# Differential attention whose key and query units hold both maps of two heads, with later projections between its rounds

## The reference

```python
kv = jnp.einsum('bsd,de->bse', kvh, w_kv)      # k1 | k2 | v, 6 heads of 64, 64 and 128
q1 = proj[..., :DIFF_QK].reshape(b, s, DIFF_HEADS, DIFF_HEAD_DIM)
q2 = proj[..., DIFF_QK:2 * DIFF_QK].reshape(b, s, DIFF_HEADS, DIFF_HEAD_DIM)
qm = proj[..., 2 * DIFF_QK:]                   # queries of the memory, 4 heads of 64
q1 = partial_rope(rmsnorm_2(q1, b_q_norm[j]), cos, sin)     # k1, k2, q2 likewise
s1 = jnp.einsum('bqhd,bkhd->bhqk', a1, k1).astype(jnp.float32) * scale
p = (p1 - lam * p2).astype(v.dtype)            # p1, p2: softmax of the maps s1, s2
o = rmsnorm_2(o, b_subln[j], SUBLN_EPS) * (1.0 - lam_init)
mo = memory_attention(qm, mem_n, w_mem_kv[l], mem_q_norm[l], mem_k_norm[l])
x = x + jnp.einsum('bse,ed->bsd', jnp.concatenate([main, mo], axis=-1), w_o[l])
```

## Time and profile before

| | us |
|---|---|
| median of 3 runs | 1164.06 |
| lowest and highest run | 1162.13, 1166.34 |
| the profiled execution, its own time | 1163.43 |
| its span | 1161.6 |
| mean granted clock of TensorE | 0.966 |

### The profile page before, as it was taken

How to read it: one execution, slowest core, us unless ns; L and a number is a source line. 1 busy time by engine, 2 the same in 40 slices (tenths; PEclk the granted TensorE clock), 3 DMA queues, 4 the chain that set the end, 5 groups by cost and what they waited for, 6 DMA issues and landing times.

```text
span 1161.6 us, 19998 instructions
## 1 busy us (share of the span) xinstructions
PE 1086.9 (94%) x8646; PEld 1061.7 (91%) x8646; DVE 650.1 (56%) x833; ACT 542.5 (47%) x770; POOL 371.0 (32%) x198
## 2 busy tenths in 40 slices
PE   6889898999899999989999999999999669999998
PEld 6889898899899999979999999999997559999998
DVE  3767755556684654555755444447555655544444
ACT  3366675543556444533355343445434334553341
POOL 2436256231464433450001341221531020252121
PEclk9989999899899999989999999999999689999999
DMA  9978457545377555434355555564433104655540
GB/s 325 279 243 254 133 165 257 171 146 177 114 250 258 181 182 179 148 121 133 111 181 199 177 190 181 173 211 163 146 114 106 36 1 146 218 182 180 183 146 37
DMA packets 167715, 197.38 MB, mean 170 GB/s; under 512 B 5283, under 2 KB 139852, under 8 KB 167500
## 3 DMA queue, kind: packets, MB, share of 16 engines
q1 hardware_dynamic: 167628, 196.11, 52.2%
HBM read 195.03 MB, written 1.06 MB: 169 GB/s over the span
## 4 chain that ended last, share of the span: by engine, by line
PE 71%; DVE 11%; ACT 8%; DMA 3%; issue 3%; POOL 2%; SPq 2%; DVEq 1%; ACTq 0%; POOLq 0%
PE bank L486 70%; DVE w_lo L1525 4%; ACT w_hi L1029 3%; DMA ada_raw<-in_w_ada 2%; ACT ada_raw L1019 2%; ACT probs L1092 1%; SPq L442 1%; DVEq L1941 1%; POOL ada_raw L1384 1%; DVE y_tok L1648 1%; DMA probsT<-in_buckets 1%; DVE big L1921 0%; DVE probs L1629 0%; DVE h_lo L1582 0%; DVE big L1747 0%
## 5 line engine op out<-in xcount | busy, mean ns | idle before, releaser
L1525 DVE TENSOR_TENSOR w_lo<-w_raw,w_hi 128x2048 fp32r<-128x2048 f32 x158 | 389.0, 2465 | 283.7 <-ACT w_hi L1029 283.1
L486 PE MATMUL bank<-h_hi,w_hi 128*128 128x256 f32 x1328 | 382.2, 293 | 13.4 <-DVE w_lo L1525 11.1
L486 PE MATMUL bank<-h_hi,w_lo 128*128 128x256 f32 x1328 | 377.3, 289 | 0.0
L1029 ACT ACTIVATE w_hi<-w_raw 128x2048 fp32r<-128x2048 f32 x158 | 301.3, 1908 | 133.0 <-PE bank L486 124.2
L486 PE MATMUL bank<-h_lo,w_hi 128*128 128x256 f32 x1328 | 346.4, 286 | 1.3 <-POOL h_lo L1353 1.3
L486 PE MATMUL bank<-u_hi,w_hi 128*128 128x256 f32 x1024 | 289.7, 286 | 8.9 <-DVE xT L1950 4.6
L486 PE MATMUL bank<-u_hi,w_lo 128*128 128x256 f32 x1024 | 287.3, 284 | 0.0
L1353 POOL TENSOR_TENSOR u_lo<-fresh,u_hi 128x512 fp32r<-128x512 f32 x60 | 139.1, 2320 | 453.0 <-ACT u_hi L1038 452.8
L486 PEld LDWEIGHTS bank<-h_hi,w_hi 128*128 128x128 f32 x1328 | 264.2, 199 | 16.6 <-DVE w_lo L1525 12.3
L486 PE MATMUL bank<-u_lo,w_hi 128*128 128x256 f32 x1024 | 277.2, 284 | 0.0
L486 PEld LDWEIGHTS bank<-h_hi,w_lo 128*128 128x128 f32 x1328 | 264.0, 199 | 0.0
(11 more groups left out here) (235 smaller groups left out, 1042.3 us busy)
## 6 DMA issues: line engine op xcount, KB each, us to landing
w_raw<-in_w_mlp SPq DMA_DIRECT2D x32, 1024.0 KB, 5.4
w_raw<-in_w_up SPq DMA_DIRECT2D x32, 1024.0 KB, 5.5
w_raw<-in_w_down SPq DMA_DIRECT2D x32, 1024.0 KB, 5.0
w_raw<-in_w_in SPq DMA_DIRECT2D x21, 1024.0 KB, 5.3
ada_raw<-in_w_ada SPq DMA_DIRECT2D x19, 1024.0 KB, 7.8
w_raw<-in_a_w_in SPq DMA_DIRECT2D x10, 1024.0 KB, 5.1
w_raw<-in_w_o SPq DMA_DIRECT2D x8, 1024.0 KB, 4.9
w_raw<-in_w_kv SPq DMA_DIRECT2D x6, 1024.0 KB, 5.3
```

Source lines behind the costliest of these rows:

```text
L486: return pe.matmul(dst, lhsT, rhs, start=start, stop=stop, skip_group_check=True)
L1029: act.activation(w_hi[:, n % PARTS_RING, :], w_raw[:, slot_of[n], :], ACT.Copy).then_inc(hi_w, 1)
L1525: dve.tensor_tensor(w_lo[:, n % PARTS_RING, :], w_raw[:, slot_of[n], :], w_hi[:, n % PARTS_RING, :].bitcast(F32), ALU.subtract).then_inc(l ...
```

## The change

A unit of keys or of queries now holds 128 columns of the first map and 128 of the second: both maps of two heads (`heads_unit`). The units come in the order k0, q0, v0, memory queries, k1, q1, v1, k2, q2, v2, and head pair 0 can start after k0 and q0. The six rounds begin there. The other units, the values and the two pairs of the memory's attention stand between the steps of the rounds, in the programs of all engines. The scores of the next round stand behind the transposition of this one, not ahead of it, and use two banks instead of four.

The gain of a key or query is applied where ACT empties the bank, the rotation follows at once, and only keys get their rstd multiplied in (`head_scale`, after the rotation). The rstd of queries (the first layer's memory queries too) goes into the scale of the exponential, and DVE multiplies it into the negated maximum. The five `spread_qk` of queries (q0, q1, q2 and both layers' memory queries) and their DVE multiplications are gone; those of the keys and of the memory's keys remain.

```diff
+    def heads_unit(name, src, pair):
+        n_unit(name, src, 0, "a", [(0, P * pair, P), (P, DIFF_HEADS * HD + P * pair, P)])
+
+    heads_unit("k", w["w_kv"], 0)
+    heads_unit("q", w["b_w_q"][0], 0)
+    n_unit("v", w["w_kv"], MAIN_W, "a")
+    n_unit("qm1", w["b_w_q"][0], MAIN_W, "a")
...
-            spread_qk("qm0", acc[3])
...
-            product_two(N_K, h_hi, h_lo, in_order(X_KV), ready=(x_hi, x_lo))
+            product(N_K[0], h_hi, h_lo, job=X_KV, ready=(x_hi, x_lo))
             sum_x("sum6")
...
+            product(N_Q[0], u_hi, u_lo, job=X_MIX1, ready=(x_hi, x_lo))
...
+            qk_squares("k0", N_K[0])
+            rotate("k0", tiles_of("k0"))
+            product_tok(N_V[0], h_hi, h_lo)
+            rotate("q0", tiles_of("q0"))
+            qk_squares("q0", N_Q[0])
+            spread_qk("k0", acc[3])
+            product(N_QM1, u_hi, u_lo)
+            d_scores(0)
+            product(N_K[1], h_hi, h_lo)
+            qk_squares("qm1", N_QM1)
+
+            d_turn(0)
+            d_scores(1)
+            qk_squares("k1", N_K[1])
+            rotate("k1", tiles_of("k1"))
+            pv(0)
+            product(N_Q[1], u_hi, u_lo)
+
+            d_turn(1)
+            spread_qk("k1", acc[3])
+            rotate("q1", tiles_of("q1"))
+            qk_squares("q1", N_Q[1])
+            pv(1)
+            turn_o(0)
+            product_tok(N_V[1], h_hi, h_lo)
+            d_scores(2)
+            product(N_K[2], h_hi, h_lo)
+
+            d_turn(2)
+            qk_squares("k2", N_K[2])
+            rotate("k2", tiles_of("k2"))
+            d_scores(3)
+            pv(2)
+            turn_o(1)
+            product(N_Q[2], u_hi, u_lo)
...
+            product_tok(N_V[2], h_hi, h_lo)
+            d_scores(4)
+            o_part(0, J_DIFF[0], first=True)
+            pe.wait_ge(spread_read, spread_no["qk.k2"] + 1)
+            m_scores(0)
+
+            d_turn(4)
+            d_scores(5)
+            pv(4)
+            turn_o(3)
+            m_turn(0)
+            m_pv(0)
+            m_scores(1)
+
+            d_turn(5)
+            m_turn(1)
+            pv(5)
+            turn_o(4)
+            m_pv(1)
+            o_part(1, J_DIFF[1])
+            pe.wait_ge(misc_read, misc_no["mem1.1"] + 1)
+            pe.wait_ge(d_max, DIFF_HEADS)
+            to_T(acc[0:1], y_tok, y_turned)
+            turn_o(5)
+            o_part(3, J_YM1)
...
+                act.activation(dst, lin[lin_bank[n]][:, :], ACT.Copy, scale=1.0 if gain is None else vec[:, gain:gain + 1])
...
+                                              scale=root[:, q_rstd:q_rstd + 1],
...
+            split_w(N_QM0)
             squares_x("sum3")
             squares_x("sum3g")
-            split_w(N_QM0)
...
+            d_exps(2)
+            split_w(N_K[2] + AHEAD)
+            evac_k(2)
+
+            d_copy(2)
+            d_exps(3)
+            o_square(2)
+            split_w(N_Q[2] + AHEAD)
+            evac_q(2)
...
+            d_copy(4)
+            d_exps(5)
+            mem_exps(0)
+            o_square(4)
+            split_w(N_V[2] + AHEAD + 1)
+            split_h(J_DIFF[1], u_hi, 2)
+            copy_turned("mem1.", 0, G_M1, 512, mem_pT)
...
+            d_maxima(2)
+            split_w(N_K[2] + AHEAD)
+            mix(2)
+
+            head_mean("k2")
+            rope_add("k2", k_pair[2])
+            d_maxima(3)
+            o_copy(2)
+            o_take(1)
+            split_w(N_Q[2] + AHEAD)
+            o_mean(2)
+            mix(3)
+            o_scale(2)
```

More of the change, by code:

```diff
@@ L650, in spread_qk @@
                 pe.wait_ge(root_ready, power_no[name] + 1)
-                if bank is ps_ada:
+                if bank is not acc[1]:
                     pe.wait_ge(spread_read, spread_no[name])
@@ new lines, in o_part @@
+            def o_part(pair, job, first=False, last=False):
+                for m in range(2):
+                    if first:
+                        start_unit(N_O1 + m)
+                    pe.wait_ge(fresh_lo, job + 1)
+                    part(N_O1 + m, pair, u_hi, u_lo, first=first, last=last)
+            qk_squares("k0", N_K[0])
[3 more added lines that the diff above has]
+            qk_squares("q0", N_Q[0])
@@ new lines, in _ @@
+            pv(3)
+            turn_o(2)
+            product_tok(N_V[2], h_hi, h_lo)
[15 more added lines that the diff above has]
+            m_pv(1)
@@ new lines, in _ @@
+            evac_q(0)
+            split_w(N_V[0] + AHEAD)
+            evac_v_unit(0)
+            split_w(N_QM1 + AHEAD)
+            evac_qk("qm1", N_QM1, v_tok[:, 0, :], gain=V_MQ + 1)
+            d_exps(0)
+            split_w(N_K[1] + AHEAD)
+            evac_k(1)
+            d_copy(0)
+            d_exps(1)
+            split_w(N_Q[1] + AHEAD)
+            o_square(0)
+            evac_q(1)
+            d_copy(1)
+            o_square(1)
+            split_w(N_V[1] + AHEAD)
+            evac_v_unit(1)
@@ L2013, in _, with head_mean @@
[L2013 to L2022 removed]
+            def head_mean(name):
+                mean_square("qk." + name, mix_eps)
@@ L2084, in o_take @@
                     dve.drain().then_inc(fresh_ready, 1)
-            y_copy(J_YM1, 0, 6)
-            split_w(N_O1 + AHEAD)
-            d_maxima(0)
-            for h in range(DIFF_HEADS):
-                mix(h)
-                if h >= 2:
-                    o_take(h - 2)
-                if h >= 1:
-                    o_mean(h - 1)
-                if h + 1 < DIFF_HEADS:
-                    d_maxima(h + 1)
-                if h >= 1:
-                    o_scale(h - 1)
-                o_copy(h)
@@ new lines, in _ @@
+            dve.tensor_scalar(stat[:, S_NLAM:S_NLAM + 1], stat[:, S_NLAM:S_NLAM + 1], -LAM_INIT, None, ALU.add)
+            head_scale(0)
+            split_w(N_V[0] + AHEAD)
+            dve.wait_ge(root_ready, power_no["qk.q0"] + 1)
+            d_maxima(0)
+            split_w(N_QM1 + AHEAD)
+            mix(0)
+            head_mean("qm1")
+            d_maxima(1)
+            split_w(N_K[1] + AHEAD)
+            head_mean("k1")
+            rope_add("k1", k_pair[1])
+            o_copy(0)
@@ new lines, in _ @@
+            split_w(N_Q[1] + AHEAD)
+            o_mean(0)
+            mix(1)
+            o_scale(0)
+            head_scale(1)
+            rope_add("q1", q_pair[1])
+            head_mean("q1")
+            o_copy(1)
+            o_take(0)
+            split_w(N_V[1] + AHEAD)
+            o_mean(1)
+            o_scale(1)
+            dve.wait_ge(root_ready, power_no["qk.q1"] + 1)
+            d_maxima(2)
+            split_w(N_K[2] + AHEAD)
+            mix(2)
+            head_mean("k2")
@@ new lines, in _ @@
+            rope_add("k2", k_pair[2])
[6 more added lines that the diff above has]
+            o_scale(2)
+            head_scale(2)
+            rope_add("q2", q_pair[2])
+            head_mean("q2")
+            o_copy(3)
+            o_take(2)
+            split_w(N_V[2] + AHEAD)
+            o_mean(3)
+            o_scale(3)
+            dve.wait_ge(root_ready, power_no["qk.q2"] + 1)
+            d_maxima(4)
@@ L2104, in _ @@
+            mix(4)
+            mem_maxima(0)
+            d_maxima(5)
+            o_copy(4)
+            o_take(3)
+            split_w(N_V[2] + AHEAD + 1)
+            o_mean(4)
+            o_scale(4)
+            mix(5)
+            attended("mem1.", 0, G_M1)
+            mem_maxima(1)
+            o_copy(5)
+            o_take(4)
+            o_mean(5)
+            o_scale(5)
+            attended("mem1.", 1, G_M1 + 1)
+            y_copy(J_YM1, 0, 6)
+            o_take(5)
             residual(N_O1, AHEAD + 1, X_H7, V_MLP + 8, last=False)
```

423 lines of the change are left out of this document (203 added, 220 removed).

## The result

| | before | changed |
|---|---|---|
| median (us) | 1164.06 | 1175.63 |
| lowest to highest of 5 runs | 1161.66 to 1166.34 | 1172.08 to 1178.24 |
| the profiled execution, its own time | 1163.43 | 1176.67 |
| its span | 1161.6 | 1174.9 |
| mean granted clock of TensorE | 0.966 | 0.952 |

The ratio is 1.0099, with a 95% interval of 1.0071 to 1.0126: slower by 1.0%. The forecast was 1174.0.

What follows compares the result with a forecast made beforehand. In the rounds a chain of small steps over four engines was taken to set the time. -1.0 - 2.5 + 13.6 = +10.1 on 1163.43 gave 1173.5, so a median of 1174 us; range 1158 to 1186.

Steps and rivals of the forecast that it cites:

- The first layer's spread: First layer, where TensorE runs through: one of five removed spreads saves its time, -1.0 us.
- The start: Before the changed stretch: nothing won, q0 ends at 821.4 where the second key unit ended at 821.1.
- TensorE's work: From 821.4 to the last w_o pieces: TensorE's busy work at full clock sums to 96.8 us.
- The waits at full clock: Same stretch: TensorE's waits for other engines, listed round by round, sum to 30.3 us.
- The clock: Three thin stretches where TensorE's clock falls to half speed: +13.6 us together.
- (b): 878 to 889 us: transposition, squares, rotation and scores at half speed on the chain to `d_maxima(3)`, +3.7 us.
- (c): 914 to 940 us, no unit left: scores, memory products, turns at half speed, less what waits absorb, +7.5 us.
- (a): 844.7 to 852.0 us: small steps and a 2.6 us wait; clock falls, q1 partly at 1.2 GHz, +2.4 us.
- The sum: Whole kernel: -1.0 first layer, -2.5 stretch at full clock, +13.6 clock, together +10.1 us on 1163.43.
- B: Rival: clock stays up between units and is low no more than before in rounds 4 and 5; 1160 us, chance 0.22.
- D: Rival: key and query loads in two 512 KB transfers come 6 us late at q1; 1180 us, chance 0.10.
- C: Rival: waits hidden better, half of the 30 us of waits and half the clock price; 1152 us, chance 0.08.

Runs made afterwards that it cites:

- the best version: Changed kernel with weight splits moved behind the rounds' steps and 148 unread matmuls in TensorE's waits, some behind the rounds; 1152.94 us, 0.9914 of the kernel before.
- the dense filling: Changed kernel in its own order with 186 unread matmuls in the stretch and 36 behind it; 1163.63 us.

## Why the prediction was right, point by point

- **The first layer's spread**: -1.0 forecast. The stage is 78.77 us where it was 79.25, so -0.5. TensorE's idle time in it is the same (6.9 us), so the other half went in slower work and not in waits; no run shows why.
- **The start**: q0 ended at 821.0 for 821.4, though it began 0.9 later. The dip of the clock that I carried over did not fall there (1.00 for 0.92): -1.3.
- **TensorE's work**: 96.8 (96.9, as six rounds of 3.25 are 19.5), or 93.9 without the memory's last 24 products. In the best version at 1.00 it is 94.5 to 96.2: 118.6 less 9.0 of idle time and 15.1 of unread matmuls by their rows, or 13.4 at 0.12 each.
- **The waits at full clock**: 30.3. With the order unchanged and the clock at 0.97 the idle time and the unread matmuls in it are 31 to 33 (8.8, and 22.3 at 0.12 each or 24.6 by their rows). In the changed kernel itself they are 24.1. One by one, forecast and measured: round 0 2.6, 2.2; round 1 1.0, 1.05 and 0.6, 0.6; round 2 3.8, 4.5; behind the rotation of q2 1.4, 2.1; rounds 4 and 5 1.4, 1.6; 1.3, 0.6; 2.3, 2.1; 3.2, 2.4; 2.8, 1.8; 0.9, 0.8 and at the end 2.4, 2.6. Three more (1.8 for `o_copy(2)`, 2.0 ahead of the transposition of round 3, 1.5 ahead of that of round 5) were 0.6, 0 and 0: in their place stood slow matmuls and a slow q2 (with q2 at full clock the wait of round 3 is there, 2.19). The reading of the series on VectorE and ScalarE was the part that held best.
- **A price left out**: the exponential's scale from a tile is not free, 0.09 each, 0.4 per round. No row of before showed that form, and the text took nothing for it. The Trainium skill, ScalarE: Activation LUTs, What ACT_TABLE_LOAD costs, says that each operand read per partition adds about 93 ns to an activation. The trace agrees, by 586 less 493; read beforehand, it would have added 0.4 to each chain of a round.
- **The clock**: +13.6, a little too high. Measured by the dense filling it is 9.3, and 12.4 with the 3.1 us of the piece that stayed low. Its places were right in (b) and (c) (0.50 in 886 to 898 and 927 to 956) and in (a) (q1 at 0.70), and in (a) and (b) so was the price: 2.7 for 2.4, with q1's extra 2.1 on the path, and 3.3 for 3.7, the small matmuls ahead of `d_maxima(3)`, as the text had it. The term that was mis-sized is (c): 1.4 and 3.1, so 4.5, in place of 7.5: the waits from the transposition of round 4 on, forecast as 16.4 at full clock, were 12.4 in the changed kernel, so that they took in about 4 us of slow matmuls. The 1.9 us between rounds 3 and 4, 1.2 of it in v2, stood on the upper side of the forecast only, and made up for a part.
- **The sum**: -2.5 and +13.6 were +11.1 for the stretch; +11.35 was measured. From the end of q0 to the last w_o pieces, 127.7 us were forecast at full clock (821.4 to 949.1), where the kernel before took 130.5 (821.1 to 951.6). With the clock held by unread matmuls it was 133.6, or 130.5 with the last low piece at full pace. The gain of 2.5 at full clock was thus not seen; a little of that is the unread matmuls' own (0.6 us ahead of the values of round 3, where they take longer than the wait that they fill). Against it stand the 1.3 of the start and 1.2 of the clock. The mechanisms were right. That the total of the stretch is off by 0.3 us, when its terms are off by 1 to 3, is luck.
- **The rivals**: B (1160 with the clock up) named the right alternative; with the clock held by added work it is 1163.6, no gain on the kernel before. D is excluded. C (1152, half of the waits and half of the clock's price) is out: reordered, the kernel still took 1166.3, and it took unread matmuls as well to reach 1152.9.

What stays open is why the clock falls at one place in one execution and not in the next (unit q0 took 5.8 us in the changed kernel's profile and 7.3 in four of those of the experiments), and so how much of the last 2 us between two medians is the edit. The scores of the next round now stand behind the transposition and share two banks; no run changed that alone, so its part in the waits is not shown.

## What to carry to other kernels

Work that is moved in between the steps of a chain in which each step waits for the one before should stand behind the steps on every engine, not only on the one that it is meant to keep busy: here the multiplications filled TensorE, but their preparation on VectorE and ScalarE stood ahead of the chain, and four reordered places were worth 9 us. Before mixing sparse and dense work on TensorE, ask which of the slowed matmuls stand on the chain, whatever their size: here slow unit q1 cost its extra 2.1 us, slow unit q2 nothing, since `mix(3)` came no earlier, and the small matmuls ahead of `d_maxima(3)` 3.3. Where the clock falls in a stretch with waits, matmuls that nothing reads are a cheap trial. They won 7 to 12 us in the changed kernel and nothing measurable in the kernel before, and one that starts at the low clock or outlasts its wait delays what follows.

## What the hardware did that I had not expected

- Holding the clock wins nothing measurable in one kernel (ratio 0.9995, 0.9978 to 1.0012, with the clock of the stretch up from 0.89 to 0.96) and 12 us in another (0.80 to 0.97 from the end of q0 on).
- Work added to TensorE made the kernel faster: 1166.29 to 1156.33 with 104 matmuls more, and to 1152.94 with 148. The Trainium skill, Perfetto Trace Analysis, Matmul Optimizations, says that the matmul engine scales its power with utilization, so that matmuls should run back-to-back in batches. These two runs agree in what they show, the granted clock (0.85 in the stretch from q0 on without the unread matmuls, 0.99 and 1.00 with them); the kernel before, with its clock held, got no faster.
- Unread matmuls begun at the low clock take longer and delay what stands behind them: 40 of them took 7.2 us, where 40 at 0.12 are 4.8, and moved the transposition of round 0 later by 2.4 us (11.5 in place of 9.1 from the first scores).
- Transfers of 512 KB in runs of 512 bytes land in 4.5 and 4.6 us, where whole units of 1 MB of the same two tensors take 5.0 and 5.3 before, and give no loss against whole units (ratio 0.9985 to 1.0016).
